# A 64-slot expert on one 64-column tile beside two 32-column tiles, in the three-expert units of a Mixture-of-Experts decoder trunk

## The chip, the cores and the metric

The kernel runs on one core of one Trainium2 chip. Its time is the device time of the whole program in microseconds (us). The core has a matrix engine (TensorE, PE in the profile; its weight loads are a row of their own, PEld), a vector engine (DVE), a scalar engine (ACT), a general one (POOL) and SyncE (SP), which here issues nearly all DMAs.

## What is computed

The reference is a decoder trunk of two layers on 256 tokens of 1024 channels, in float32. Each layer has a token mixer (a gated short convolution in layer 0, a chunked causal gating MLP in layer 1), a residual LayerNorm, a Mixture of Experts, and another residual LayerNorm. The Mixture of Experts is what matters here:

```python
def moe(x, ...):                      # x: 256 tokens x 1024
    # 64 experts, top 8 of each token, one shared expert
    scores = sigmoid(x @ router_w); top_e = ...; gate = ...
    for each expert e:
        h = x[tokens of e]
        y = (silu(h @ w_gate[e]) * (h @ w_up[e])) @ w_down[e]   # 1024->256, 1024->256, 256->1024
        routed[tokens of e] += gate * y
    return routed + shared
```

Every expert has three matrices of 1 MB each, and all 64 are read in each layer.

## The kernel before

**Slots and units.** Experts are sorted by how many tokens they have. The largest get 64 slots each (`WIDE`), the others 32 (`NARROW`). Work goes in rounds of two units, and each unit fills the 128 output partitions of the matrix engine. Round 0 has four experts of 64 slots. In each of the rounds 1 to 12 the even unit has three experts, of which the first has 64 slots and the others 32 each, and the odd unit has two experts of 64 slots. The function `tiles_of(u)` lists, for unit u, which expert's weights go with which range of slots; each entry is one matmul of that width in slots. So a unit is cut into two column tiles of 64, or four column tiles of 32. In the three-expert unit the 64-slot expert k stands there twice.

**Matmuls of a unit.** The gathered tokens are the stationary operand (one column for each slot), the weights are the moving operand, and each entry of `tiles_of` writes its own range of PSUM partitions. `gate_up` (matmul at L896) goes over 8 chunks of the 1024 channels; for each chunk it issues one matmul for each entry, with 512 moving columns (gate and up side by side). For the last rounds (from unit `LAST + 2` = 22 on) `gate_side` and `up_side` call `one_side` (L908), which does the same in two passes over the chunks with 256 moving columns. `down` (L947) has 2 halves of 2 chunks each, again one matmul of 512 columns for each entry. All these are float32, and each float32 matmul is two LDWEIGHTS and two MATMUL records of the trace: one chunk of four tiles is 8 MATMUL records, one of two tiles 4.

```python
for c in chunks:
    for k, first, width in tiles_of(u):
        last = nc.tensor.matmul(ps[first:first + width, p, :],
                                xsT[:, c, p * P + first:p * P + first + width],
                                gate_up_of(layer, k, c), start=(c == 0), stop=(c == KC - 1))
```

**Order on the matrix engine in rounds 2 to 11.** `gate_up` of the even unit; `combine` of the unit before (L964, adds outputs back to tokens) in two parts with `turn` (L931, transposes the hidden values) between; `down` of the even unit; `gate_up` of the odd unit; `combine`, `gather` (L875, picks the next round's tokens by a 0/1 matrix) and `turn`; `down` of the odd unit. Waits for weights stand in front of `gate_up` and `down`.

**Weights.** The ring has 6 slots of one expert each. SP waits for `gu_done` of a unit and then issues gate and up matrices for the experts that take over its slots; then it waits for `y_done` of that unit and issues their down matrices (`refill`, `last_refills`). All goes through one queue in a fixed order. `experts_of`, the ring slots and this order depend only on which experts stand in `tiles_of`, not on how they are cut into tiles.

**The other engines** in a unit: ACT takes the sigmoid from PSUM (L1306), DVE makes the hidden values (L1669, L1672), ACT and DVE split the output in high and low parts (L1315, L1683), and DVE adds up (L1692).

Of the kernel before, what the change touches and what calls it, by code (L numbers as in the profile page):

```python
# [44 lines left out]
WIDE = 64  # L45
NARROW = 32
# [42 lines left out]
def first_of(r):  # L89

    return 0 if r == 0 else FIRST + PER_ROUND * (r - 1)


def tiles_of(u):

    k = first_of(u // 2)
    if u == 0:
        return [(k, 0, WIDE), (k + 1, WIDE, WIDE)]
    if u == 1:
        return [(k + 2, 0, WIDE), (k + 3, WIDE, WIDE)]  # L100
    if u % 2 == 0:
        return [(k, 0, NARROW), (k, NARROW, NARROW), (k + 1, 2 * NARROW, NARROW), (k + 2, 3 * NARROW, NARROW)]
    return [(k + 3, 0, WIDE), (k + 4, WIDE, WIDE)]


def experts_of(u):
    return sorted({k for k, _, _ in tiles_of(u)})
# [88 lines left out]
def build(nc, x, xT0, a_w_in, a_conv_w, a_w_out, b_w_in, b_ln, b_wsT, b_w_out, rows, router_w,  # L196
          router_bias, w_gate, w_up, w_down, sh_gate, sh_up, sh_down, out):
    ctx = ExitStack()
    with ctx:
# [538 lines left out]
        def _(pe):  # L738
# [148 lines left out]
            def gate_up(layer, r, p, chunks=range(KC)):  # L887
                W, u = L[layer], 2 * r + p
                for k in experts_of(u):
                    pe.wait_ge(gate_load[slot_of(layer, k)], gate_up_ready(layer, k))  # L890
                    pe.wait_ge(up_load[slot_of(layer, k)], gate_up_ready(layer, k))
                for c in chunks:
                    if r <= 1 and p == 0 and c % 2 == 0:
                        pe.wait_ge(W.xs_ready, W.past.xs_ready + 4 * r + c // 2 + 1)
# [4 lines that stand above are left out]
                    if u < len(PARTS) and c + 1 in [used for _, used in PARTS[u][:-1]]:  # L899
                        last.then_inc(W.part_used, 1)  # L900
                if chunks[-1] == KC - 1:
                    last.then_inc(W.gu_done, 1)

            def one_side(layer, u, side, chunks):
                p = u % 2
                for c in chunks:
                    for k, first, width in tiles_of(u):
                        last = nc.tensor.matmul(ps[first:first + width, p, side * H:(side + 1) * H],  # L908
                                                xsT[:, c, p * P + first:p * P + first + width],
                                                gate_up_of(layer, k, c)[:, side], start=(c == 0), stop=(c == KC - 1))  # L910
                return last
# [1058 lines left out]
```

## Time and profile before

| | |
|---|---|
| time before, median of 3 runs | 1292.08 us (1290.05 to 1293.18) |
| the profiled execution's own time | 1292.19 us |
| span of the profiled execution | 1290.5 us |
| PE busy | 1204.3 us, 93% |
| DVE, ACT, POOL busy | 568.2, 376.8, 15.8 us |
| DMA | 473.87 MB, mean 367 GB/s |
| granted TensorE clock, mean | 0.988 of full |
| three-expert units, four tiles of 32 | 24 (12 in each layer) |

Read the first two lines together: the span leaves out 1.7 us around it. PE is the busiest engine, but its busy time counts all tiles that run at once as one stretch, and a record's end is modelled. The DMA line is a mean over stages that differ; the rows by stage are below.

### The profile page before, as it was taken

To read this page: it belongs to the slowest core of one execution; us is meant where nothing else is said; L and a number is where in the kernel's file an instruction comes from. 1 tells how busy PE (TensorE), PEld (TensorE's weight loads), DVE (VectorE), ACT (ScalarE), POOL (GpSimd) and SP (SyncE) were. 2 spreads that over 40 slices of the span, in tenths; PEclk is the share of its full clock that TensorE was granted. 3 is DMA by queue.
4 is the path that set the end of the run, shared out by engine and by line. 5 is a ranking of instruction groups with operands and counts; after the bars stand their busy time and mean duration, and the time that the engine had idled before them with its cause. 6 is when DMAs were issued, how large, how long until landed. Compare 5 with 4: busy or idle time off the path is not lost.

```text
span 1290.5 us, 20282 instructions
## 1 busy us (share of the span) xinstructions
PE 1204.3 (93%) x7916; PEld 737.8 (57%) x7916; DVE 568.2 (44%) x1265; ACT 376.8 (29%) x673; POOL 15.8 (1%) x32
## 2 busy tenths in 40 slices
PE   8999999999888988989999999999999888789897
PEld 7986444444334444559999998644444444244464
DVE  5756443333233223328676666634333333233233
ACT  4443221222022222315454443322222221122221
POOL 0001000000000000000000000000000000000000
PEclk9999999999899999999999999999999999999999
DMA  9977999999999999999635435899999999999996
GB/s 302 389 300 312 382 418 420 414 421 421 420 421 421 421 420 421 421 411 401 261 144 185 158 148 236 327 416 419 416 410 420 421 421 421 420 422 421 420 420 247
DMA packets 92481, 473.87 MB, mean 367 GB/s; under 512 B 8160, under 2 KB 23648, under 8 KB 46560
## 3 DMA queue, kind: packets, MB, share of 16 engines
q1 hardware_dynamic: 90320, 469.79, 90.0%
q10 hardware_dynamic: 2064, 2.75, 0.6%
q8 instruction: 65, 1.06, 0.3%
q14 instruction: 32, 0.26, 0.1%
HBM read 471.46 MB, written 1.05 MB: 366 GB/s over the span
## 4 chain that ended last, share of the span: by engine, by line
PE 63%; DMA 28%; DVE 3%; SPq 3%; issue 1%; ACT 1%; POOL 0%; DVEq 0%; ACTq 0%
DMA ring<-in_w_up 23%; PE ps L896 18%; PE ps L776 10%; PE ps L947 7%; PE ps L788 6%; PE ps L818 5%; PE ps L875 4%; PE ps L908 3%; PE ps L964 3%; SPq L493 2%; PE ps L986 2%; DMA ring<-in_w_gate 2%; DMA ring<-in_w_down 2%; PE ps L994 1%; PE ps L863 1%
## 5 line engine op out<-in xcount | busy, mean ns | idle before, releaser
L896 PE MATMUL ps<-ring,xsT 128*32 128x512 f32 (+1 forms) x2048 | 327.0, 612 | 53.5 <-DMA ring<-in_w_up 53.5
L896 PEld LDWEIGHTS ps<-ring,xsT 128*32 128x32 f32 (+1 forms) x2048 | 105.8, 123 | 266.0 <-issue 264.6
L947 PE MATMUL ps<-ring,hidT 128*32 128x512 f32 (+1 forms) x1200 | 189.7, 596 | 6.0 <-DMA ring<-in_w_down 5.8
L1669 DVE SCALAR_TENSOR_TENSOR sig<-sig,slot_gate,ps 128x256 f32<-128x256 f32 x52 | 25.0, 480 | 363.9 <-ACT sig L1306 363.9
L1458 DVE TENSOR_TENSOR ring_low<-ring,wh 128x1024 fp32r<-128x1024 f32 (+1 forms) x111 | 127.4, 1148 | 88.4 <-ACT wh L1230 87.6
L1230 ACT CAST wh<-ring 128x1024 fp32r<-128x1024 f32 (+1 forms) x111 | 109.5, 988 | 145.8 <-PE ps L776 64.6
L1692 DVE TENSOR_TENSOR X<-X,ps 128x512 f32<-128x512 f32 x184 | 118.3, 682 | 52.2 <-PE ps L964 37.5
L1306 ACT ACTIVATE sig<-ps 128x256 f32<-128x256 f32 x52 | 20.0, 384 | 401.4 <-PE ps L896 347.7
L1683 DVE TENSOR_TENSOR yl<-ps,yh 128x512 fp32r<-128x512 f32 x104 | 71.5, 691 | 132.4 <-ACT yh L1315 132.4
L1294 ACT ACTIVATE xsT<-ps,cols 128x256 f32<-128x256 f32 x208 | 102.4, 560 | 83.1 <-PE ps L875 83.1
L947 PEld LDWEIGHTS ps<-ring,hidT 128*32 128x32 f32 (+1 forms) x1200 | 53.2, 119 | 103.3 <-issue 102.6
L1315 ACT CAST yh<-ps 128x512 fp32r<-128x512 f32 x104 | 60.5, 586 | 175.1 <-PE ps L947 155.3
L776 PE MATMUL ps<-xTh,wh 128*128 128x256 f32 x376 | 105.5, 281 | 1.4 <-DVE ring_low L1458 1.4
L776 PE MATMUL ps<-xTl,wh 128*128 128x256 f32 x376 | 105.5, 281 | 0.0
L776 PE MATMUL ps<-xTh,ring_low 128*128 128x256 f32 x376 | 105.4, 280 | 0.0
L875 PE MATMUL ps<-sel,xh 128*128 128x256 f32 x416 | 105.4, 293 | 0.0
L875 PE MATMUL ps<-sel,xl 128*128 128x256 f32 x416 | 100.7, 281 | 0.0
L964 PE MATMUL ps<-yh,back 128*128 128x512 f32 x184 | 83.0, 451 | 4.0 <-DVE X L1692 4.0
L875 PEld LDWEIGHTS ps<-sel,xh 128*128 128x128 f32 x416 | 78.9, 190 | 4.0 <-issue 2.6
L875 PEld LDWEIGHTS ps<-sel,xl 128*128 128x128 f32 x416 | 78.8, 190 | 2.3 <-issue 1.4
L964 PE MATMUL ps<-yl,back 128*128 128x512 f32 x184 | 72.9, 396 | 0.0
L776 PEld LDWEIGHTS ps<-xTh,wh 128*128 128x128 f32 x376 | 70.7, 188 | 2.8 <-DVE ring_low L1458 1.8
(219 smaller groups left out, 1388.2 us busy)
## 6 DMA issues: line engine op xcount, KB each, us to landing
ring<-in_w_gate SPq DMA_DIRECT2D x128, 1024.0 KB, 21.3
ring<-in_w_down SPq DMA_DIRECT2D x126, 1024.0 KB, 24.7
ring<-in_w_up SPq DMA_DIRECT2D x124, 1024.0 KB, 23.6
ring<-in_b_w_in SPq DMA_DIRECT2D x8, 3072.0 KB, 25.7
ring<-in_b_w_out SPq DMA_DIRECT2D x4, 3072.0 KB, 11.0
ring<-in_a_w_in SPq DMA_DIRECT2D x9, 1024.0 KB, 12.0
ring<-in_w_up SPq DMA_DIRECT2D x8, 512.0 KB, 24.2
ring<-in_a_w_out SPq DMA_DIRECT2D x1, 3072.0 KB, 18.0
```

Of the source, the lines that this page charges most:

```text
L776: last = nc.tensor.matmul(dst, a[:, c, :], b[:, c, :], start=(c == 0 and b is xTh and a is wh_n), stop=(c == KC - 1 and a is wl_n))
L788: last = nc.tensor.matmul(ps[:, 4 + 2 * t + h, :], a[:, t * P:(t + 1) * P], b[:, cols], start=False, stop=(n == len(PIECES[layer]) - 1 and ...
L818: last = nc.tensor.matmul(ps[:, first + m, 0:384], a[:, c, t * P:(t + 1) * P], b[:, cols], start=(c == 0 and a is xTh and b is wh_n), stop ...
L875: last = nc.tensor.matmul(dst, part[:, t, c, :], sel[:, t, :], start=(n == 0), stop=(n == 3))
L896: last = nc.tensor.matmul(ps[first:first + width, p, :], xsT[:, c, p * P + first:p * P + first + width], gate_up_of(layer, k, c), start=(c ...
L947: last = nc.tensor.matmul(ps[first:first + width, 4 + h, :], hidT[:, p, kk * P + first:kk * P + first + width], down_of(layer, k)[:, kk, h ...
L964: last = nc.tensor.matmul(dst, back[:, p, t * P:(t + 1) * P], part[:, h * HALF:(h + 1) * HALF], start=(part is yh), stop=(part is yl and s ...
L1230: nc.scalar.copy(wh_n, w).then_inc(L[layer].wh_ready, 1)
L1294: return nc.scalar.activation(dst, src, ACT.Identity, bias=cols[:, 4 * layer + 1, c:c + 1], scale=cols[:, 4 * layer, c:c + 1])
L1458: nc.vector.tensor_tensor(wl_n, w, wh_n.bitcast(FP32), ALU.subtract).then_inc(L[layer].wl_ready, 1)
L1683: nc.vector.tensor_tensor(yl[:, cols], ps[:, 4 + h, :], yh[:, cols].bitcast(FP32), ALU.subtract).then_inc(W.yl_ready, 1)
L1692: nc.vector.tensor_tensor(X[:, t, cols], X[:, t, cols], ps[:, 2 + h, :], ALU.add).then_inc(W.comb_taken, 1)
```

## The change

In `tiles_of`, the even units from 2 on get three entries in place of four. The first expert's 64 slots become one column tile of 64; the other two experts keep their tiles of 32. Units 0 and 1 and all odd units stay as they are.

```diff
@@ -99,7 +99,7 @@
     if u == 1:
         return [(k + 2, 0, WIDE), (k + 3, WIDE, WIDE)]
     if u % 2 == 0:
-        return [(k, 0, NARROW), (k, NARROW, NARROW), (k + 1, 2 * NARROW, NARROW), (k + 2, 3 * NARROW, NARROW)]
+        return [(k, 0, WIDE), (k + 1, 2 * NARROW, NARROW), (k + 2, 3 * NARROW, NARROW)]
     return [(k + 3, 0, WIDE), (k + 4, WIDE, WIDE)]
```

All of `gate_up`, `one_side` and `down` go over `tiles_of(u)`, so in these 24 units each chunk has one matmul fewer: 64, then 32, then 32 slots, then the next chunk's 64 again.

## Rows read from the trace of the kernel before

**Rows 1.** The profile page: span, DMA total, and the span in 40 slices.

```profile
span 1290.5 us, 20282 instructions
...
PEclk9999999999899999999999999999999999999999
...
GB/s 302 389 300 312 382 418 420 414 421 421 420 421 421 421 420 421 421 411 401 261 144 185 158 148 236 327 416 419 416 410 420 421 421 421 420 422 421 420 420 247
```

**Rows 2.** PE's groups by shape: count | busy us, mean ns of one | idle before.

```profile
L896 PE MATMUL ps<-ring,xsT 128*64 128x512 f32 x768 | 183.8, 633 | 35.0 <-DMA ring<-in_w_up 34.9
L896 PE MATMUL ps<-ring,xsT 128*32 128x512 f32 x1280 | 143.2, 599 | 18.5 <-DMA ring<-in_w_up 18.5
...
L947 PE MATMUL ps<-ring,hidT 128*32 128x512 f32 x768 | 87.4, 595 | 5.6 <-DMA ring<-in_w_down 5.6
...
L908 PE MATMUL ps<-ring,xsT 128*32 128x256 f32 x512 | 28.9, 380 | 1.7 <-DMA ring<-in_w_up 1.7
```

**Rows 3.** Windows over rounds: us, then busy us of each engine, PEclk, DMA share, GB/s.

```profile
229.47:260.48 31.01, 30.48 (x203) 13.83 (x201) 11.91 (x30) 7.79 (x16) 0.00 (x0) 1.00 1.00 414
291.48:513.40 221.92, 193.50 (x1202) 89.96 (x1200) 71.47 (x180) 46.74 (x96) 0.00 (x0) 0.95 1.01 421
932.89:963.88 30.99, 30.46 (x202) 13.82 (x200) 11.91 (x30) 7.79 (x16) 0.00 (x0) 1.00 0.99 409
994.89:1215.78 220.89, 188.69 (x1202) 89.22 (x1200) 71.47 (x180) 46.74 (x96) 0.00 (x0) 0.98 1.01 421
513.40:545.61 32.21, 31.69 (x302) 18.87 (x300) 12.30 (x31) 8.38 (x17) 0.00 (x0) 1.00 1.01 421
```

**Rows 4.** PE's waits over the whole span: us in total, times, longest.

```profile
PE ps L896 <- DMA ring<-in_w_up: 53.5, 22, 3.7
PE ps L931 <- DVE hid L1672: 8.1, 24, 0.4
PE ps L947 <- DMA ring<-in_w_down: 5.8, 5, 2.9
...
PE ps L908 <- DMA ring<-in_w_up: 1.7, 2, 1.4
```

**Rows 5.** Windows on the matmuls of L896: two-tile and four-tile units, the last row after a wait.

```profile
243.50:251.70 8.20, 7.04 (x32) 2.16 (x32) 1.00 1.01 423
260.50:268.50 8.00, 7.05 (x64) 1.95 (x64) 1.00 1.01 420
...
494.69:502.92 8.23, 8.23 (x32) 3.11 (x32) 0.79 1.01 417
```

**Rows 6.** Timeline, from 64-slot tiles (`down`) to 32-slot tiles (`gate_up`).

```profile
259.95 0.60 PE L947 MATMUL ps<-ring,hidT 128*64 128x512 f32 x2
260.48 0.16 PEld L896 LDWEIGHTS ps<-ring,xsT 128*32 128x32 f32 x8 [0.81 <-issue]
260.48 1.50 PE L896 MATMUL ps<-ring,xsT 128*32 128x512 f32 x12
...
260.93 0.13 PEld L896 LDWEIGHTS ps<-ring,xsT 128*32 128x32 f32 x4 [0.30 <-issue]
...
261.36 0.13 PEld L896 LDWEIGHTS ps<-ring,xsT 128*32 128x32 f32 x4 [0.30 <-issue]
```

**Rows 7.** Timeline, from 32-slot tiles (`down`) to 64-slot tiles (`gate_up`).

```profile
242.93 0.60 PE L947 MATMUL ps<-ring,hidT 128*32 128x512 f32 x2
243.45 0.20 PEld L896 LDWEIGHTS ps<-ring,xsT 128*64 128x64 f32 x4 [0.84 <-issue]
...
243.94 0.14 PEld L896 LDWEIGHTS ps<-ring,xsT 128*64 128x64 f32 x2 [0.29 <-issue]
244.37 0.14 PEld L896 LDWEIGHTS ps<-ring,xsT 128*64 128x64 f32 x2 [0.29 <-issue]
```

## The prediction

> **What bounds the kernel now.** I read the page first, then PE's groups by shape, then windows cut at the start of each round, then PE's waits, and last the timeline at a fine grain where the tile width changes. The page [rows 1] shows two expert stages, one in each layer, in which the queue moves 420 GB/s or so, and a slow stage between them (layer 1's mixer) which this change does not touch. The windows by round [rows 3] show what sets the pace. A round takes 31.0 us where PE never waits (layer 0, round 3; the same in layer 1), and PE is busy for 30.5 of it. A round needs 5 experts x 3 matrices of 1 MB, 15.7 MB, which at 421 GB/s is 37.3 us. So PE runs ahead of the queue at first, uses up the weights that were loaded before, and from the sixth round on waits for weights: six rounds from 291.48 to 513.40 take 221.9 us, and six in layer 1 take 220.9, against 6 x 31.0 = 186. The slack of PE is therefore 35.9 + 34.9 = 70.8 us in these twelve rounds. The waits [rows 4] say what it is: 53.5 us on an up matrix in front of L896, and 5.8 + 1.7 us in front of L947 and L908, mostly in the last two rounds. The remainder is clock: a unit that begins after such a wait takes 8.23 us at a mean granted clock of 0.79 where its like takes 7.04 at 1.00 [rows 5]. Waits are 61 us in all, slow stretches some 17, so about 78 us would be given back if the queue were never late. That 78 is the cushion for any work added to PE; beyond it each microsecond on PE is a microsecond of the result.
>
> **What the change removes.** In 24 units it removes one tile of four: of 1280 records of L896 with 32 slots a quarter goes, and the same of L947 and L908 [rows 2]. That is worth nothing by itself. Four tiles of 32 and two tiles of 64 take the same time for 8 chunks, 7.05 and 7.04 us [rows 5], though one has 64 records and the other 32. The rows of weight loads show why [rows 6, 7]: in a steady stretch they come in bundles, four (or two) every 0.43 us, one bundle for each of the two passes of a float32 matmul. The tiles of a chunk stream side by side, so a chunk costs 2 x 0.43 = 0.86 us however many tiles it has, as long as they run together.
>
> **What it adds.** The question is whether a tile of 64 and a tile of 32 run together. No place of the trace has them on separate columns. What it has are places where the width changes, and two things are seen there. First, the new width starts late: from the last bundle of 64-slot matmuls at 259.95 to the first of 32 at 260.48 is 0.53 us [rows 6], and from 32 to 64 it is 242.93 to 243.45, 0.52 us [rows 7], against the 0.43 within one width. Second, the weights of the new width are not loaded ahead: their load begins with the matmul itself (both passes' loads, 8 or 4, stand at that moment), and the second pass comes 0.45 us later for 32 slots [rows 6], 0.49 for 64 [rows 7]. PE behaves as if it had to be empty before it takes another width. All columns were occupied at these places, so the delay alone does not prove that a tile on free columns would wait too; but weights of the old width are loaded ahead of running matmuls while those of the new width are not, and I read that as a barrier for everything of the other width. I take it that the two widths take turns.
>
> The Trainium skill, page "TensorEngine Tiling (Array Packing)", section "Key Properties", states this as a rule: changing the tiling mode, and not only the tile, drains the engine. The extra tenth of a microsecond in the rows agrees with it; by that rule the sum is the one below.
>
> With turns, a chunk goes: 64-slot pass one to pass two, 0.49; to the 32-slot pair, 0.53; their pass one to two, 0.45; back to 64, 0.52. Together 1.99 us against 0.86, so 1.13 more. Of this 4 x 0.43 = 1.72 is streaming and 0.27 is changing. With 256 moving columns (L908) streaming is half, so a chunk costs 0.86 + 0.27 = 1.13 against 0.43, 0.70 more.
>
> Chunks: in each layer ten three-expert units have 8 chunks in `gate_up` and 4 in `down`, and two have 16 half-wide chunks in `one_side` and 4 in `down`. So 10 x 12 + 2 x 4 = 128 full chunks and 32 half-wide ones: 128 x 1.13 + 32 x 0.70 = 144.6 + 22.4 = 167.0 us for a layer, 334 us for both.
>
> **Is PE then the bound everywhere?** A round becomes 31.0 + 12 x 1.13 = 44.6 us, more than the 37.3 that the queue needs, so the waits on weights should go, with the slow stretches behind them: -78 us. Nothing else moves. SP waits for `gu_done` and `y_done` of these units, which come 9.0 us later (8 x 1.13) and then 4.5 more; the queue then idles at times, and its share falls. The followers of a unit's slots are needed a round later, and in that round the queue has seven microseconds more than it needs, so I see no new wait for weights. The sigmoid, hidden and split steps of ACT and DVE start later but take no longer; their PE wait (8.1 us over 24 units [rows 4]) stays. The combine, gather and turn matmuls keep their places.
>
> The sum is 1292.2 (the profiled execution's own time; its span is 1290.5, and the median of the runs is 1292.08, so no correction) + 334 - 78 = **1548 us**.
>
> **Bounds of the added cost.** Below: the widths take turns but a change costs nothing, so a chunk is 1.72 us; 128 x 0.86 + 32 x 0.43 = 123.8 a layer, 248 - 78 = +170, 1462 us. The extra 0.10 us at each change is in the rows, so I expect to be above that; if also a round's margin over the queue got thin (41.3 against 37.3) waits would hardly return. Above: each change also exposes a whole weight load, 0.14 us [rows 7], since alternating tiles can prefetch nothing; a chunk is then 2.27 us and a half-wide one 1.41, 128 x 1.41 + 32 x 0.98 = 212 a layer, 424 - 78 = +346, 1638 us. Between them I take the rows of the changes as they are, since they are the very sequence (64 to 32 to 64) that will be repeated.
>
> **Rivals.** (A) is the forecast: turns, 1548.
>
> (B) The widths run side by side as equal widths do. Then a chunk of three tiles costs 0.86 us, PE's work is the same to 0.01 us a unit (7.05 against 7.04 [rows 5]), and the time is 1292. For it speaks that the tiles are separate in columns and that the number of tiles has no effect on the time of a chunk; against it the missing load-ahead at each change of width. The Trainium skill, page "TensorE: Matmul & The Clock Gate", Part 3 ("Measured speedup vs the span model"), gives packed matmuls as one duration plus about 4 ns for each further tile and makes no exception for unequal tiles; by that rule alone it would be this case. The rows agree with it for equal tiles and show nothing for unequal ones.
>
> (C) They overlap, but weights are not loaded ahead across widths. A chunk then costs 0.86 + 2 x 0.14 = 1.14 us, a round 31.0 + 12 x 0.28 = 34.4 us, still under 37.3. The queue stays the bound in the later rounds and hides it there; only about the first three rounds, in which the queue has no hold on PE, and the last two, where PE ends the stage, show it partly, some 4 us a layer: 1300 us.
>
> (D) Faster: the 64-slot expert's weights are streamed once, not twice, and this frees the engine's read side so that the chunk of three tiles gets shorter. It decides from 0.33 us a unit over the twelve units of round 1 to 3 and of the last three rounds in both layers, since the rounds between are held by the queue; that gives the 3.9 us (0.3%) needed, 1288 us. Against it: two tiles with half the streams are 0.01 us faster for 8 chunks than four [rows 5].
>
> **How the numbers follow.** A has 0.84, B 0.10, C 0.04, D 0.02. From 1440 to 1640 holds nearly all of A (1462 to 1638, with 20 us below for the cushion, which may be larger if other rounds gain clock), about 0.80 in all. It leaves out B, C and D. A measurement of this kernel can tell about 0.3% (3.9 us) from no change. Slower by more is A and C, 0.88; within is B, 0.10; faster D, 0.02.
>
> **What the profile after will show.** If A holds: the 32-slot rows of L896 halve to 640 and 64-slot rows grow by 320; on the timeline a three-expert unit alternates one 64-slot bundle pair and one 32-slot bundle pair, eight times, in some 16 us in place of 7; `down` of that unit takes 8 us in place of 3.6; rounds are 44 to 45 us long; the wait for an up matrix in front of L896 is gone, PEclk is 1.00 in these stages, and GB/s there falls from 421 to about 15.7 MB / 44.6 us = 353. If B: all is as before but for counts. What would make A wrong in size: changes that cost more when they come every half microsecond than once in a unit, weights loaded ahead after all, a clock that falls because half of the columns are idle at any time (seen in no row here), or a chain of slots in which the queue's idle stretches come back as waits on PE.

## The result, and the profile after

The changed kernel takes 1537.62 us (1537.23 to 1538.07, 4 runs) against 1291.07 us (1289.91 to 1293.18) of the kernel before: a ratio of 1.191, 95% interval [1.1895, 1.1925]. The profiled execution took 1537.94 us, 1.8 of them around its span.

The page of the changed kernel, to hold against [rows 1]:

```profile
span 1536.1 us, 19002 instructions
...
PE 1510.2 (98%) x7276; PEld 751.8 (49%) x7276; DVE 568.2 (37%) x1265; ACT 376.8 (25%) x673; POOL 15.9 (1%) x32
...
PEclk9999999999999999999999999999999999999999
...
GB/s 307 398 318 307 311 296 326 364 348 349 344 352 348 358 409 332 293 183 401 211 115 166 177 188 342 376 317 322 267 343 352 382 390 347 350 347 340 284 352 28
```

There are 640 fewer MATMUL records on PE and it is busy 306 us longer. DVE and ACT do what they did. The queue moves some 350 GB/s in most slices of the expert stages, where it moved 421. The chain that ended last has 93% on PE and 1% on DMA, where it had 63% and 28%.

PE's groups by shape in the changed kernel, to hold against [rows 2]:

```profile
L896 PE MATMUL ps<-ring,xsT 128*64 128x512 f32 x1088 | 341.1, 601 | 0.1
L947 PE MATMUL ps<-ring,hidT 128*64 128x512 f32 x624 | 205.2, 604 | 0.9 <-ACT hidT L1310 0.9
L896 PE MATMUL ps<-ring,xsT 128*32 128x512 f32 x640 | 168.3, 605 | 0.0
```

Half of the 32-slot records of L896 are gone, and the half that is left keeps PE busy longer (168.3 us) than all of them did (143.2). A busy time here is the union of overlapping records, so this says that fewer of them overlap. PE's waits in the changed kernel have no wait for weights left, in these lines or in L908.

The timeline of weight loads in a three-expert unit of the changed kernel, to hold against [rows 6]:

```profile
299.97 0.14 PEld L896 LDWEIGHTS ps<-ring,xsT 128*64 128x64 f32 x1 [0.29 <-issue]
300.92 0.14 PEld L896 LDWEIGHTS ps<-ring,xsT 128*32 128x32 f32 x4 [0.81 <-issue]
301.90 0.19 PEld L896 LDWEIGHTS ps<-ring,xsT 128*64 128x64 f32 x2 [0.84 <-issue]
302.90 0.14 PEld L896 LDWEIGHTS ps<-ring,xsT 128*32 128x32 f32 x4 [0.81 <-issue]
303.89 0.19 PEld L896 LDWEIGHTS ps<-ring,xsT 128*64 128x64 f32 x2 [0.84 <-issue]
```

The widths take turns. From one bundle of 64-slot loads to the next is 1.99 us, one chunk; it was 0.86. Each bundle holds the loads of both passes, and it comes about 0.52 us after the last pass of the other width has started (300.40 to 300.92, and 301.38 to 301.90), so nothing is loaded ahead across the change. The two stretches of the unit and a round, by timeline and windows of the changed kernel:

```profile
299.97 15.90 PE L896 MATMUL ps<-ring,xsT 128*64 128x512 f32 x48
...
319.19 8.01 PE L947 MATMUL ps<-ring,hidT 128*64 128x512 f32 x24
```

```profile
327.12:371.19 44.07, 43.55 (x178) 15.01 (x176) 11.91 (x30) 7.79 (x16) 0.00 (x0) 1.00 0.87 359
```

`gate_up` takes 15.90 us in place of 7.05 [rows 5], `down` 8.01 in place of 3.64 (L947 at 270.89 of the kernel before). The round takes 44.07 us in place of 31.01 [rows 3] in the rounds that the queue did not hold, and in place of some 37 (221.92 / 6) in those that it did. The eight rounds of layer 0 from round 3 on are alike now for PE: each takes 44.07 us at a granted clock of 1.00. The queue is busy for 0.73 of the first of them and for 0.85 to 0.88 of the others.

### The profile page after: what moved, and what is told of

Same layout as the page of the kernel before. It is cut to its first block, busy times and chain, and to the rows that moved or that the text cites. A ratio compares the mean times of both kernels' runs of the same rounds, so it can differ in the third digit from the quotient of the medians.

```text
span 1536.1 us, 19002 instructions
## 1 busy us (share of the span) xinstructions
PE 1510.2 (98%) x7276; PEld 751.8 (49%) x7276; DVE 568.2 (37%) x1265; ACT 376.8 (25%) x673; POOL 15.9 (1%) x32
## 4 chain that ended last, share of the span: by engine, by line
PE 93%; DVE 4%; ACT 1%; issue 1%; DMA 1%; POOL 0%; SPq 0%; DVEq 0%; ACTq 0%
PE ps L896 32%; PE ps L947 19%; PE ps L776 8%; PE ps L908 7%; PE ps L875 6%; PE ps L788 5%; PE ps L964 5%; PE ps L818 4%; PE ps L986 2%; PE ps L994 1%; DVE X L1692 1%; DVE sig L1669 1%; PE ps L863 1%; DVE hid L1672 1%; ACT sig L1306 1%
## 5 line engine op out<-in xcount | busy, mean ns | idle before, releaser
L896 PE MATMUL ps<-ring,xsT 128*64 128x512 f32 (+1 forms) x1728 | 488.6, 602 | 0.1
L947 PE MATMUL ps<-ring,hidT 128*64 128x512 f32 (+1 forms) x1008 | 294.5, 604 | 0.9 <-ACT hidT L1310 0.9
L896 PEld LDWEIGHTS ps<-ring,xsT 128*64 128x64 f32 (+1 forms) x1728 | 108.3, 125 | 368.4 <-issue 367.5
L947 PEld LDWEIGHTS ps<-ring,hidT 128*64 128x64 f32 (+1 forms) x1008 | 61.7, 125 | 194.3 <-issue 192.3
L908 PE MATMUL ps<-ring,xsT 128*64 128x256 f32 (+1 forms) x640 | 101.1, 389 | 0.0
```

Source lines behind the costliest of these rows:

```text
L896: last = nc.tensor.matmul(ps[first:first + width, p, :], xsT[:, c, p * P + first:p * P + first + width], gate_up_of(layer, k, c), start=(c ...
L947: last = nc.tensor.matmul(ps[first:first + width, 4 + h, :], hidT[:, p, kk * P + first:kk * P + first + width], down_of(layer, k)[:, kk, h ...
```

## The experiments

Six kernels were run, each beside the kernel before on the same chip. The medians of the kernel before in these runs are 1291.22 us for the first four and 1290.69 for the last two.

**Three tiles of equal width.** Is it the unequal width, or only that there are three tiles? Here the second tile of 32 of the unit's 64-slot expert is left out, so that three tiles of 32 remain. The kernel leaves out slots 32 to 63 of that expert and so computes less than the others; it serves to time three equal tiles.

```diff
-        return [(k, 0, NARROW), (k, NARROW, NARROW), (k + 1, 2 * NARROW, NARROW), (k + 2, 3 * NARROW, NARROW)]
+        return [(k, 0, NARROW), (k + 1, 2 * NARROW, NARROW), (k + 2, 3 * NARROW, NARROW)]
```

> The three-expert units run three tiles of 32 columns (slots 32 to 63 of their largest expert are left out, so less is computed), everything else is as before. Theory 1, unequal widths take turns: three equal tiles stream side by side, a chunk costs 0.86 us, the time is that of the kernel before, 1291 us within 3. Rival 1, it is the odd number of tiles, or the missing fourth one, that breaks the overlap: chunks as long as in the changed kernel, 1500 us or more. Rival 2, fewer streams are faster: below 1287.

It took 1290.67 us against 1291.22, ratio 0.9999 [0.999, 1.0008]. The window over the same `gate_up` as before shows 48 records in the time of 64:

```profile
229.48:236.60 7.12, 7.06 (x48) 1.87 (x48) 1.00 1.01 422
```

So three tiles overlap as four do, and from two to four tiles the number of streams has no price and no gain in a chunk. Rival 1 falls, and so does the "faster" mechanism (D) of the prediction, that fewer streams shorten a chunk.

**The order turned round in every odd chunk.** Two chunks then meet at one width, which takes away about half of the changes of width and nothing of the turns. The three-expert unit's `down` also ends on its 64-slot tile now, so `gate_up` of the next unit begins without a change wherever it follows at once (18 times).

```diff
+def snake(u, c):
+    return tiles_of(u) if c % 2 == 0 else tiles_of(u)[::-1]
...
-                    for k, first, width in tiles_of(u):
+                    for k, first, width in snake(u, c):
```

The same edit stands in `gate_up`, `one_side` and `down`, on the changed kernel.

> The changed kernel with the order of tiles turned round in every odd chunk (64, 32, 32, then 32, 32, 64), so that two chunks meet at one width. Streaming in turns is the same; changes of width inside a three-expert unit fall from 15 to 8 in gate_up, from 7 to 4 in down, from 31 to 16 in the half-wide form. Theory 1, turns plus some 0.134 us for each change (a stretch of 8 chunks of the changed kernel takes 15.31 us from its first to its last start, 31 x 0.429 + 15 x 0.134): gate_up 14.4 us from first to last start, 1500 us in all. Rival, changes cost nothing and only the streaming in turns counts: gate_up still 15.3, and 1538. Rival 3, the engine looks past a waiting tile when the next equal tile is near: more overlap and below 1480.

It took 1499.08 us (1498.96 and 1499.20), ratio 1.161 [1.1589, 1.1631]. A `gate_up` takes 14.97 us: its first record starts at 253.30, and the timeline row of the others is

```profile
253.73 14.54 PE L900 MATMUL ps<-ring,xsT 128*64 128x512 f32 x47
```

**All of one width first.** The 64-slot tile goes through all its chunks, then the two 32-slot tiles through theirs.

```diff
+def widths_of(u):
+    return sorted({w for _, _, w in tiles_of(u)}, reverse=True)
...
-                for c in chunks:
+                for group, c in [(w, c) for w in widths_of(u) for c in chunks]:
...
                     for k, first, width in tiles_of(u):
+                        if width != group:
+                            continue
```

> The changed kernel with all chunks of the 64-slot tile first and then all chunks of the two 32-slot tiles: one change of width in gate_up, three in down and in the half-wide form. Theory 1: gate_up 31 x 0.429 + 0.134 = 13.4 us from first to last start, down 6.8, half-wide form 14.0; 1472 us. Rival, the whole cost is in the changes and nothing in the turns: gate_up about 6.6 us and about 1292. Rival 3, tiles of different width overlap once the weights are there: second width starts early, below 1400.

It took 1471.99 us (1471.59 and 1472.40), ratio 1.14 [1.138, 1.1421]. The timeline shows `gate_up` whole, and then the one place where it changes width:

```profile
250.97 14.02 PE L902 MATMUL ps<-ring,xsT 128*64 128x512 f32 x48
```

```profile
257.40 1.57 PE L902 MATMUL ps<-ring,xsT 128*64 128x512 f32 x5
257.93 0.14 PEld L902 LDWEIGHTS ps<-ring,xsT 128*32 128x32 f32 x4 [0.81 <-issue]
258.38 0.12 PEld L902 LDWEIGHTS ps<-ring,xsT 128*32 128x32 f32 x2 [0.31 <-issue]
```

The columns of the 32-slot tiles have had nothing to do for 6.9 us here, and their tokens and weights are there. Most of that time says nothing about widths: the program has the 32-slot matmuls behind the last 64-slot one, and how far the engine would look past a waiting matmul was not measured. By that order a `gate_up` without a barrier would be only some 0.5 us shorter (an estimate: one change at 0.53 in place of the 0.01 between tiles of one width). What counts is the last step. The last 64-slot pass starts at 257.40, and the first load of the other width comes at 257.93, 0.53 us later, though the columns it needs are free. This is the piece that no row of the kernel before could show: free columns do not help a tile of another width.

**Narrow tiles everywhere.** The opposite of the change: the two-expert units too are cut into tiles of 32.

```diff
-    return [(k + 3, 0, WIDE), (k + 4, WIDE, WIDE)]
+    return [(k + 3 + n // 2, n * NARROW, NARROW) for n in range(4)]
```

> The kernel before with the two-expert units of rounds 1 to 12 cut into four tiles of 32 too, so that no width but 32 (and 128) is left there. Theory 1: a chunk costs 0.86 us for any number of equal tiles, and one change of width a unit of 0.1 us goes; rounds that the queue does not hold get 0.1 to 0.3 us shorter, 1290 to 1291 us, not to be told from before. Rival, twice the weight loads and matmuls cost something: more than 0.1 us a unit, 1294 or more.

It took 1293.05 us (11 runs) against 1291.22, ratio 1.0013 [1.0004, 1.0022]. The theory was right for the units: from the last start of `down` to the first of `gate_up` is 0.41 us (228.87 to 229.28) in place of 0.53 (228.94 to 229.47), and a round that the queue does not hold takes 30.70 us in place of 31.01.

```profile
229.28:259.98 30.70, 30.17 (x253) 13.67 (x249) 11.91 (x30) 7.79 (x16) 0.00 (x0) 1.00 1.01 414
```

But the whole is 0.13% longer, 1.8 us, which it did not foresee; the rival's price of more than 0.1 us a unit is not it either, since a round got shorter. The profiled executions, whose spans differ by 1.1 us, show where it comes from. Near the end of layer 1 PE is still ahead of the kernel before (L742 starts at 1264.07 against 1264.38). Then the last unit waits 1.60 us for its gate matrix, where the kernel before waited 0.16, and its L908 starts at 1266.83 against 1265.70. Why that matrix lands later was not found.

**Unequal widths in `gate_up` only**, and **in `down` only.** These two ask what becomes of added work: the first lifts a round above the pace of the queue, the second leaves it below. In each of them one of the functions goes over the four tiles of before, kept as `narrow_tiles_of`:

```diff
-                        for k, first, width in tiles_of(u):
+                        for k, first, width in narrow_tiles_of(u):
                             last = nc.tensor.matmul(ps[first:first + width, 4 + h, :],
```

> Unequal widths in gate_up and its half-wide form only; down of the three-expert units keeps four tiles of 32. Theory 1: by the stretches of the changed kernel each of 20 full units takes 8.83 us more (15.31 against 6.48) and each of 4 half-wide ones 11.0, 220.6 us in all; a round is 39.9 us, above the queue's 37.3, so the whole cushion of 80 us is given back: 1433 us. Rival, waits on weights come back since a round is only 2.6 us over the queue: up to 20 us more, 1450.

It took 1432.80 us (1432.63 and 1432.97), ratio 1.11 [1.1078, 1.1123].

> Unequal widths in down only: 24 units x 4.37 us = 104.9 us more work on PE; a round is 35.4 us, still under the queue's 37.3. Theory 1, added work is hidden up to the cushion: the queue holds the later rounds, the rounds before them and the last two show it; 1291 + 105 - 80 at the least, with some waits left 1317 to 1328. Rival, added work is never hidden: 1396. Rival 2, the queue hides all of it: 1291 to 1295.

It took 1318.70 us (4 runs) against 1290.69, ratio 1.0216 [1.0199, 1.0234]. Windows over one round of the first, and over two rounds of the second:

```profile
286.83:326.53 39.70, 39.18 (x186) 14.62 (x184) 11.91 (x30) 7.79 (x16) 0.00 (x0) 1.00 0.96 397
```

```profile
237.84:273.20 35.36, 34.83 (x194) 14.22 (x192) 11.91 (x30) 7.79 (x16) 0.00 (x0) 1.00 0.92 371
273.20:308.56 35.36, 34.84 (x195) 14.23 (x193) 11.90 (x30) 7.79 (x16) 0.00 (x0) 1.00 1.01 420
```

In the second the queue is full in every round of layer 0 from 273 us on (a share of 1.01 in each of the next seven), and yet PE waits for no weights at all: its largest wait is that on DVE's hidden values.

```profile
PE ps L938 <- DVE hid L1679: 8.0, 24, 0.3
PE ps L971 <- DVE X L1699: 4.1, 22, 0.2
```

A round of 35.36 us asks only 1.9 us more of the queue than it can give, 19 us over ten rounds. I conclude that what was loaded ahead at the start lasts that long; the lead itself was not traced. So the net price, 28.0 us, is the added work of 104.9 (24 x 4.37) less 76.9: nearly the full cushion, though a round is shorter than the queue's 37.3. Neither "all hidden" nor "never hidden" holds.

## Why the prediction was right, point by point

**The bound before: right.** PE's work and the queue's pace lie close together. The two half experiments show the exchange from both sides. With `gate_up` alone, 142.1 us net for about 221 added: 79 given back, of which 2 are the entries named under the size below. With `down` alone, 104.9 - 28.0 = 77. The forecast had 78.

**Widths take turns: right, and now shown.** It was inferred from a late start and from weights not loaded ahead, at places where all columns were busy. Three equal tiles cost 7.06 us and the three unequal ones 15.90, and in the grouped order a tile on free columns waits out the last 0.53 us. B (side by side) and C (only the load-ahead lost) are out by these runs: the second would have left a chunk at 1.14 us, and it is 1.99.

The Trainium skill's rule, page "TensorEngine Tiling (Array Packing)", section "Key Properties", that changing the tiling mode drains the engine, agrees with the grouped run (0.53 us from the last start of one width to the first of the other, beside 0.43 within one). The span rule of the Trainium skill's page "TensorE: Matmul & The Clock Gate", Part 3, agrees with the three equal tiles and is off by more than a factor of two for tiles of unequal width (7.06 and 15.90 us).

**The split between turns and changes: right.** Three orders of the same matmuls differ in the number of changes of width, here for `gate_up`:

| order | changes in `gate_up` | `gate_up`, us | whole time, us | expected |
|---|---|---|---|---|
| by chunk (the change) | 15 | 15.90 | 1537.62 | 1548 |
| turned round in odd chunks | 8 | 14.97 | 1499.08 | 1500 |
| by width | 1 | 14.02 | 1471.99 | 1472 |
| equal tiles (before) | 0 | 7.05 | 1291.22 | |

Between the first three each change costs (15.90 - 14.02) / 14 = 0.134 us. Without changes 13.89 us would be left, so of the 8.85 us that a `gate_up` got longer 6.8 are turns and 2.0 are changes. The whole times fall in line with it. The order by width has 488 changes fewer in the whole kernel, worth 65.4 us, and gained 65.6. The turned order has 272 fewer, worth 36.4 us, and gained 38.5; the 18 units that now follow a `down` without a change, at 0.1 us each, are most of the other 2. The forecast's lower bound, turns with free changes, was 1462.

**The size: 10 us too high, and the step is the count of changes.** The sum took a full chunk of 1.99 us with two changes for each chunk. A stretch of 8 chunks has only 15 changes inside, one of 4 chunks 7. That is 6.4 us in 48 stretches (48 x 0.134), and rounding a chunk up to 1.13 us makes most of the other 2. So `gate_up` gained 8.85 us, not 9.04; `down` 4.37, not 4.52; the half-wide form 11.0 (18.12 against 7.11), not 11.2. That makes 20 x 8.85 + 24 x 4.37 + 4 x 11.0 = 325.9 us in place of 334. Both errors push the same way, so the close forecast does not rest on two that cancel. The remainder is in the cushion: 1292.2 + 325.9 - 1537.9 = 80.2 us were given back in place of 78, and about 2 of them are the entry to the three-expert unit, which follows on a 64-slot `down` and now begins with its own width (20 entries x 0.1 us, not all 24, since four follow on 128-column matmuls; the gap is the 0.43 of one width, 299.54 to 299.97). With them taken off, the cushion is the forecast's 78. By the medians, 1291.07 and 1537.62, it is 77, as in the two half experiments.

**Nothing new to wait for: right.** Waits on weights are gone from all three lines, no slice of the clock row is under 9 tenths, GB/s fell to 359 in a round where 353 was forecast from the bytes, and a round is 44.07 us against 44.6.

## What to carry to other kernels

In this kernel (float32, tiles of 64 and 32 columns, two to four of them) a chunk of column tiles costs one stream, however many tiles it holds, as long as all have one width. Tiles of the other width among them are paid as a stream of their own, plus 0.134 us at each change. So cut a wide operand into tiles of its narrow neighbours' width, even if the same data is then streamed twice: 7.05 us against 7.04 for 8 chunks. Other widths and types were not run. And before you price added work on an engine that waits now and then, take its waits as a sum over the stage, not round by round: with `down` alone, 77 us came back from that sum, though a single round stayed shorter than the queue's. There the added work was larger than the sum; what a smaller addition costs was not run.

## What the hardware showed that was not expected

With the order turned round, the last tile of `down` (64 slots) and the first of the next unit's `gate_up` that has free columns start together, across two lines of the program, with earlier instructions still to come (timeline of that kernel):

```profile
278.12 0.13 PEld L951 LDWEIGHTS ps<-ring,hidT 128*64 128x64 f32 x1 [0.84 <-issue]
278.13 0.13 PEld L900 LDWEIGHTS ps<-ring,xsT 128*64 128x64 f32 x1
278.13 0.64 PE L900 MATMUL ps<-ring,xsT 128*64 128x512 f32 x1
...
278.60 0.59 PE L951 MATMUL ps<-ring,hidT 128*64 128x512 f32 x1
```

The second pass of `down`'s last matmul starts at 278.60, 0.47 us after `gate_up`'s first, though the program has it ahead. The trace does not name columns. By the program the early one must be `gate_up`'s second tile, since its first needs the columns that `down` still holds. So here a tile of equal width started as soon as its own columns allowed, 0.01 us after the one before it and past a matmul that waited for other columns. It makes the barrier between widths stand out: same width and free columns, 0.01 us; other width and free columns, 0.53 us.
